# First attention's bias rows by one product, and another order of exponentials, scores and taps, in a two-block transformer kernel

## The chip, the cores and the metric

The kernel runs on one core of one Trainium2 chip. The metric is the device time of one execution in microseconds (us). Before the change three runs took 2164.03, 2169.14 and 2170.22 us; their median is 2169.14 us.

## The reference

The reference computes two transformer blocks on 512 tokens of width 1024, in float32. The first block mixes a sliding-window attention (8 query heads, 2 key heads, blocks of 128 queries against at most 256 keys) with a gated causal convolution of 31 taps over 512 channels, then a feed-forward layer. The second block (sparse attention, spatial gating, a layer of 16384 experts) is not touched by the change. What matters here of the first block:

```python
bucket = t5_causal_bucket(jnp.maximum(dist, 0))
bias = rel_bias.astype(jnp.float32)[bucket]
...
s = jnp.where(valid[None, :, None, None], s + bias, -jnp.inf)
m = jnp.maximum(jnp.max(s, axis=-1, keepdims=True), sink)
p = jnp.exp(s - m)
denom = jnp.sum(p, axis=-1, keepdims=True) + jnp.exp(sink - m)
p = (p / denom).astype(v.dtype)
o = jnp.einsum("bnhgqk,bnkhd->bnqhgd", p, vb)
...
h = a * jax.nn.sigmoid(gate)
h = lax.conv_general_dilated(h, conv_dw[:, None, :], ...) + conv_dw_b
```

The bias of a head depends only on the distance of query and key, so one row of 384 values per head holds all of it, and a query's bias is that row shifted.

## The kernel before, in words

Activations are kept transposed, channels on partitions and the 512 tokens along the free axis, as a high and a low float32r half. Every weight comes in units of 512 KB, through a ring of three: SyncE loads a unit into `wraw` (L1001 to L1008), ScalarE casts the high half to `WH` (L1191, when the unit before the last has been begun), VectorE or GpSimd subtracts to get the low half `WL` (L2297, L1140), and TensorE does three matmuls for each 128 rows of it (L469, L472, L473). A unit of a projection has 8 times 3 matmuls of 512 tokens. Each engine runs its own list in order and waits on semaphores. PSUM has eight banks, handed out in turn by `take`: a bank is used again when the eighth product before it has been read.

**The order around the change, on TensorE.** The first three input projections (convolution gates and values of chunks 0 and 1) run by halves of the tokens. Then come the bias rows (L588), the value unit of chunk 1, two units each of chunks 2 and 3, keys, values, and four query units. Then attention (L661): scores of blocks 0 and 1; then for each of the four blocks the tap products of the last channel chunk (`last_chunk_taps`, 8, 8, 8 and 7 products with diagonal matrices), scores of the block after next, and `weighted_values`, which transposes the probabilities (L636) and multiplies them by the values (L645). Behind it the mean over channels (L682) begins the convolution's layer norm.

**The bias rows.** VectorE spreads the table `relb` (33 x 8) to `relbB` (33 x 8 x 128) at L1761, 128 copies for each head. TensorE multiplies, head by head, 128 equal columns with the one-hot matrix `oneh` (33 x 384) at L592: all 128 partitions get the row of that head. ScalarE copies each of the eight banks to `brow` (L1263), which lies in the buffer of the scores. SyncE waits for all eight, writes them to DRAM as `skew_rows` (L1026, 1536 KB), waits until they have landed, and reads them back into `biasT` with a step of one row less one element (L1029), which shifts the row of partition p by p. Only then does it issue the load of the seventh unit and those behind it.

**VectorE.** From the first projection on it runs the convolution of chunks 0 to 2, one tap an instruction (`tap`, L1776 on): taps of chunk 0 alone at first, then pairwise with the next chunk's. Before every sixth tap it makes the low half of one unit, for the ten units from chunk 2's gate to the last query unit. `gated` (L1767) multiplies a chunk's values by its gates first; for the last chunk, whose taps TensorE does, it comes early in chunk 1's second half. 77 taps come before attention, 16 inside it, four a block. In attention (L1808) VectorE's order is `logits` of block 0 (scaled scores plus bias L1821, maximum L1826), then for each block: `logits` of the next, `normalise` (L1838), the taps, the sum of the last chunk's taps (L1852, L1855), and the low half of the block before's output (L1845).

**ScalarE.** In attention (L1296), for each block: exponentials with their sums, head by head (L1302), the diagonal matrices for later taps (L1292), the copies of the transposed probabilities (L1311), and the output's high half (L1315). VectorE's `normalise` waits for the exponentials; TensorE's transposes wait for `normalise`; its weighted values wait for the copies.

Of the kernel before, what the change touches and what calls it, by code (L numbers as in the profile page):

```python
# [8 lines left out]
F32 = mybir.dt.float32  # L9
# [7 lines left out]
P = 128  # L17
T = 512
NT = T // P
# [13 lines left out]
KF = FF // P  # L33
SKEW = 3 * P

GR = 4
# [100 lines left out]
def block_pair_kernel(nc, A, onehot_rows, inv_freq, out):  # L137

    ctx = ExitStack()
    with ctx:  # L140
# [151 lines left out]
        with ExitStack() as sc:  # L292
            hpad = sb("hpad", [P, CC, TAPS - 1 + T], F32, sc)
            cacc = sb("cacc", [P, CC, T], F32, sc)
            sg = sb("sg", [P, 2, T], F32, sc)
            kk = sb("kk", [P, T], F32, sc)
            vT = sb("vT", [P, T], F32, sc)
            v1 = sb("v1", [P, NT, P], F32, sc)
            q1 = sb("q1", [P, 4, T], F32, sc)
            biasT = sb("biasT", [P, NH, 2 * P], F32, sc)  # L300
            sc1 = sb("sc1", [P, 2, NH, 2 * P], F32, sc)
            pT1 = sb("pT1", [P, NH, 2, P], F32, sc)
            sinkb = sb("sinkb", [P, NH], F32, sc)
            st1 = sb("st1", [P, 2, 8, NH], F32, sc)
            relb = sb("relb", [BUCKETS + 1, NH], F32, sc)
            relbB = sb("relbB", [BUCKETS + 1, NH, P], F32, sc)
            oneh = sb("oneh", [BUCKETS + 1, SKEW], F32, sc)
            cln = sb("cln", [P, 2, T], F32, sc)
# [3 lines left out]
        TAP_GROUPS = [(0, 8), (8, 16), (16, 24), (24, TAPS)]  # L312
        brow = sc1[:, :, :, :].rearrange("p a h n -> p (a h n)")[:, 0:NH * SKEW].rearrange("p (h n) -> p h n", h=NH)
        skew_dram = nc.dram_tensor("skew_rows", (P, NH, SKEW), F32).ap()

# [135 lines left out]
        def _(pe):  # L451
# [136 lines left out]
            def bias_rows():  # L588
                pe.wait_ge(s("relb_spread"), 1)
                for h in range(NH):  # L590
                    out = take("brow", h)
                    full(pe.matmul(out[:, 0:SKEW], relbB[:, h, :], oneh[:, :], start=True, stop=True), "brow", h)  # L592

# [33 lines left out]

            def weighted_values(b):
                kts = [1] if b == 0 else [0, 1]
                pe.wait_ge(s("probs"), b + 1)  # L630
                for i in range(NH // 2):
                    out = take("pT", b, i)
                    for j in range(2):
                        for kt in kts:
                            w = (kt if b else 0) * P
                            mm = pe.transpose(out[:, (2 * j + kt) * P:(2 * j + kt + 1) * P],  # L636
                                              sc1[:, b % 2, 2 * i + j, w:w + P], ident[:, :])
                    full(mm, "pT", b, i)
                out = take("o", b)
                for h in range(NH):  # L640
# [20 lines left out]
            def attention():  # L661
                scores(0)
                scores(1)
                for b in range(NT):
                    last_chunk_taps(b)
                    if b + 2 < NT:
                        scores(b + 2)
                    weighted_values(b)
# [332 lines left out]
        def _(sp):  # L1001
# [21 lines left out]

            for h in range(NH):
                wait_read(sp, ("brow", h))
            sp.dma_start(skew_dram, brow[:, :, :]).then_inc(s("skew_out"), 16)  # L1026
            sp.wait_ge(s("skew_out"), 16)
# [149 lines left out]
        def _(act):  # L1177
# [82 lines left out]
            def bias_rows():  # L1260
                for h in range(NH):
                    src = wait_full(act, ("brow", h))
                    act.activation(brow[:, h, :], src[:, 0:SKEW], ACT.Copy).then_inc(frees(("brow", h)), 1)  # L1263

# [31 lines left out]
            def attention():  # L1296
                for b in range(NT):
                    w = P if b == 0 else 2 * P
                    st = st1[:, b % 2]
                    act.wait_ge(s("sink_gap"), b + 1)  # L1300
                    for h in range(NH):
                        act.activation(sc1[:, b % 2, h, 0:w], sc1[:, b % 2, h, 0:w], ACT.Exp, bias=st[:, 1, h:h + 1],  # L1302
                                       accum_out=st[:, 2, h:h + 1])
                    act.activation(st[:, 4, :], st[:, 3, :], ACT.Exp).then_inc(s("exps"), 1)
                    last_chunk_diags()
                    for i in range(NH // 2):
# [356 lines left out]
        def _(dve):  # L1663
# [82 lines left out]
            def prepare():  # L1746
# [13 lines left out]
                dve.wait_ge(s("relb_landed"), 32)  # L1760
                dve.tensor_copy(relbB[:, :, :], relb[:, :].unsqueeze(2).to_broadcast([BUCKETS + 1, NH, P])).then_inc(  # L1761
                    s("relb_spread"), 1)

            def convolution():
# [29 lines left out]
                alone = TAPS // 2  # L1794
                for w in range(alone):
                    tap(0, w)
                for c in range(CC - 2):
                    for w in range(alone, TAPS):
                        tap(c, w)
                        if w - alone < alone:  # L1800
                            tap(c + 1, w - alone)
                        if c == CC - 3 and w == alone:
                            gated(CC - 1)
                for u in beside:
                    low(u, s("w_beside"))
                return lambda w: tap(CC - 2, w), range(alone, TAPS)

            def attention(tap, taps_left):  # L1808
# [50 lines left out]
                for b in range(NT):  # L1859
                    if b + 1 < NT:  # L1860
                        logits(b + 1)
                    normalise(b)
                    for w in taps_left[b * len(taps_left) // NT:(b + 1) * len(taps_left) // NT]:
                        tap(w)
                    last_chunk(b)
# [592 lines left out]
```

## Time and profile before

| what | value |
|---|---|
| median of 3 runs | 2169.14 us |
| lowest and highest run | 2164.03, 2170.22 us |
| span of the profiled execution | 2161.6 us (its own time is not listed apart) |
| TensorE busy | 2121.7 us, 98% of the span |
| VectorE, GpSimd, ScalarE busy | 1442.4, 1038.6, 858.3 us |
| mean granted TensorE clock | 0.996 of 2.4 GHz |

The span runs from the first to the last instruction of the profiled execution. TensorE's busy time counts matmuls whose ends are modelled, so that it reads high; where it waits, and at which clock it runs, tells more than its share. DVE is VectorE, ACT is ScalarE, PE is TensorE, POOL is GpSimd, SPq is SyncE's queue.

### The profile page before, as it was taken

The numbers are of one execution on the slowest core, as the hardware profiler recorded it, in microseconds if no ns is written. First come the engines' busy times: TensorE is split into PE (matmuls) and PEld (weight loads), VectorE is DVE, ScalarE is ACT, GpSimd is POOL, SyncE is SP. The second block draws the span as 40 slices with busy tenths as digits, with TensorE's granted clock in tenths as the row PEclk, the third lists the DMA queues.
The fourth block names the chain that finished last, engine by engine and source line by source line (L and its number), as shares of the span: only waits on it lengthen the run. The fifth ranks groups of instructions, "written<-read, shape, count | busy, mean of one in ns | idle before, by whom it ended". The sixth has DMA issues, their size and how long they took to land.

```text
span 2161.6 us, 29125 instructions
## 1 busy us (share of the span) xinstructions
PE 2121.7 (98%) x10648; PEld 1837.8 (85%) x10648; DVE 1442.4 (67%) x2713; ACT 858.3 (40%) x1306; POOL 1038.6 (48%) x573
## 2 busy tenths in 40 slices
PE   8989999999999999999999999999999999999999
PEld 7857888888877877899999999999998888888887
DVE  5973411110054995369998777787867999999987
ACT  4354522232264454253334444444433333333332
POOL 1203244443423333435566888888863444444342
PEclk9999999999999999999999999999999999999999
DMA  4202344444442222334347899998899999999996
GB/s 177 82 27 62 104 117 127 117 119 115 117 118 74 86 71 77 117 106 121 112 147 207 242 267 321 284 315 249 261 309 318 388 388 371 373 375 377 369 359 251
DMA packets 240489, 444.14 MB, mean 205 GB/s; under 512 B 102459, under 2 KB 152028, under 8 KB 240220
## 3 DMA queue, kind: packets, MB, share of 16 engines
q1 hardware_dynamic: 152060, 299.07, 41.8%
q0 software_dynamic: 55488, 134.83, 19.3%
q10 hardware_dynamic: 32800, 8.39, 1.8%
q8 instruction: 85, 1.39, 0.3%
q14 instruction: 56, 0.46, 0.1%
HBM read 397.71 MB, written 44.50 MB: 205 GB/s over the span
## 4 chain that ended last, share of the span: by engine, by line
PE 69%; POOL 13%; DVE 8%; issue 4%; DMA 3%; ACT 2%; SPq 0%; DVEq 0%; ACTq 0%; POOLq 0%
PE bank L469 22%; PE bank L473 22%; PE bank L472 22%; POOL gate_matrices L1151 9%; POOL y L1160 4%; DMA y<-in_peer_u_rows,gidx 3%; DVE m L1979 1%; PE bank L923 1%; DVE xn L1980 1%; DVE WL L2297 1%; PE bank L645 1%; DMA wraw<-in_peer_u 1%; ACT sc L1302 1%; DVE y L2308 0%; DVE hots L2329 0%
## 5 line engine op out<-in xcount | busy, mean ns | idle before, releaser
L1140 POOL TENSOR_TENSOR WL<-wraw,WH 128x1024 fp32r<-128x1024 f32 x171 | 435.9, 2552 | 723.5 <-ACT WH L1191 723.5
L1191 ACT ACTIVATE WH<-wraw 128x1024 fp32r<-128x1024 f32 x411 | 435.0, 1060 | 627.4 <-PE bank L469 393.6
L469 PE MATMUL bank<-XH,WH 128*128 128x384 f32 (+2 forms) x1864 | 668.8, 359 | 12.6 <-DVE WL L2297 7.8
L473 PE MATMUL bank<-XH,WL 128*128 128x384 f32 (+2 forms) x1864 | 657.8, 353 | 0.0
L472 PE MATMUL bank<-XL,WH 128*128 128x384 f32 (+2 forms) x1864 | 657.6, 353 | 0.0
L469 PEld LDWEIGHTS bank<-XH,WH 128*128 128x128 f32 x1864 | 351.4, 189 | 46.3 <-issue 12.9
L472 PEld LDWEIGHTS bank<-XL,WH 128*128 128x128 f32 x1864 | 351.6, 189 | 29.0 <-issue 0.7
L473 PEld LDWEIGHTS bank<-XH,WL 128*128 128x128 f32 x1864 | 351.1, 188 | 28.7
L2297 DVE TENSOR_TENSOR WL<-wraw,WH 128x1024 fp32r<-128x1024 f32 x240 | 293.0, 1222 | 57.6 <-ACT WH L1191 51.8
L469 PE MATMUL bank<-WH,GH 128*128 128x512 f32 x768 | 298.9, 389 | 1.6 <-issue 1.6
L473 PE MATMUL bank<-WH,GL 128*128 128x512 f32 x768 | 298.8, 389 | 0.0
L472 PE MATMUL bank<-WL,GH 128*128 128x512 f32 x768 | 298.8, 389 | 0.0
L1160 POOL DMA_INDIRECT y<-in_peer_v,gidx x128 | 185.2, 1447 | 220.7 <-DVE hN L2316 203.0
L1151 POOL DMA_INDIRECT gate_matrices<-scat_gate,scat_at x128 | 243.7, 1904 | 40.9 <-issue 38.4
L2308 DVE CUSTOM_DVE_ANT_0 y<-y,x_nat 128x1024 f32<-128x1024 f32 x128 | 156.0, 1223 | 108.6 <-DMA y<-in_peer_u_rows,gidx 103.4
L1160 POOL DMA_INDIRECT y<-in_peer_u_rows,gidx x128 | 169.3, 1323 | 106.1 <-DVE gdot L2308 77.0
L469 PEld LDWEIGHTS bank<-WH,GH 128*128 128x128 f32 x768 | 144.1, 188 | 32.3 <-issue 2.3
L473 PEld LDWEIGHTS bank<-WH,GL 128*128 128x128 f32 x768 | 144.1, 188 | 29.9
L472 PEld LDWEIGHTS bank<-WL,GH 128*128 128x128 f32 x768 | 144.2, 188 | 29.8
L2316 DVE SCALAR_TENSOR_TENSOR hN<-y,gdot,hN 128x1024 f32<-128x1024 f32 x128 | 163.9, 1280 | 3.6 <-DMA y<-in_peer_v,gidx 0.6
L1589 ACT ACTIVATE ac<-bank 128x384 f32<-128x384 f32 x122 | 59.8, 490 | 239.0 <-PE bank L473 223.6
L1904 DVE TENSOR_TENSOR y<-bank,y 128x512 f32<-128x512 f32 x22 | 15.2, 692 | 208.2 <-PE bank L473 208.2
(313 smaller groups left out, 2561.8 us busy)
## 6 DMA issues: line engine op xcount, KB each, us to landing
wraw<-in_peer_u SPq DMA_DIRECT2D x128, 512.0 KB
wraw<-in_peer_v SPq DMA_DIRECT2D x128, 512.0 KB
activations<-ac SPq DMA_DIRECT2D x122, 192.0 KB
ar<-activations SPq DMA_DIRECT2D x122, 192.0 KB
gr<-gate_matrices SPq DMA_DIRECT2D x124, 128.0 KB
wraw<-in_w_gate SPq DMA_DIRECT2D x22, 512.0 KB
wraw<-in_w_up SPq DMA_DIRECT2D x22, 512.0 KB
wraw<-in_w_down SPq DMA_DIRECT2D x22, 512.0 KB
```

The lines of the kernel that those rows point to most:

```text
L469: mm = pe.matmul(out, wh, xh, start=first, stop=False)
L472: pe.matmul(out, wh, xl, start=False, stop=False)
L473: return pe.matmul(out, wl, xh, start=False, stop=last)
L645: mm = pe.matmul(out[half, (h % 4) * P:(h % 4 + 1) * P], v1[:, b - 1 + kt, half], pT1[:, h, kt, :], start=kt == kts[0], stop=kt == 1)
L1140: pool.tensor_tensor(WL[:, u % NW, 0:m], wraw[:, u % NR, 0:m], WH[:, u % NW, 0:m].bitcast(F32), ALU.subtract).then_inc(s("w_lo"), 1)
L1151: pool.indirect_dma_start(out=gate_cells[:, :], out_offset=bass.IndirectOffsetOnAxis(ap=scat_at[:, k:k + 1], axis=0), in_=scat_gate[:, k:k ...
L1160: pool.indirect_dma_start(out=gathered[:, row % NGATHER, :], out_offset=None, in_=(u_rows if row < HS else v_rows)[:, :], in_offset=bass.I ...
L1191: act.activation(WH[:, u % NW, 0:k * n], wraw[:, u % NR, 0:k * n], ACT.Copy).then_inc(s("w_hi"), 1)
L1589: act.activation(ac[:, x % NAC, :] if x < SENT else kept[:, x - SENT, :], src[:, 0:TD], ACT.Gelu_apprx_tanh).then_inc(frees(("a", x)), 1)
L2297: dve.tensor_tensor(WL[:, u % NW, 0:k * n], wraw[:, u % NR, 0:k * n], WH[:, u % NW, 0:k * n].bitcast(F32), ALU.subtract).then_inc(made, 1)
L2308: dve.tensor_tensor_reduce(out=at, in0=at, in1=x_nat[:, :], scale=1.0, scalar=0.0, op0=ALU.mult, op1=ALU.add, accum_out=gdot[:, row:row + ...
L2316: dve.scalar_tensor_tensor(out=hN[:, NTD, :], in0=at, scalar=gdot[:, row - HS:row - HS + 1], in1=hN[:, NTD, :], op0=ALU.mult, op1=ALU.add) ...
```

## The change

The table is spread to 33 x 16 x 8, so that 128 columns hold all eight heads sixteen times. One product gives the row of head h on every partition 8c + h, one copy brings it to `brow` (128 x 384), and one DMA writes each partition's row eight times, to fill the same 128 x 8 x 384 array in DRAM; the read back is as before. In attention, ScalarE runs the exponentials of block b + 1 before its other work of block b. TensorE transposes the probabilities of block b before the scores of block b + 2. VectorE does 66 single taps before attention and 27 inside it (6, 7, 7 and 7), and gates the last channel chunk after the 37th tap. Seven PSUM banks fewer are taken.

```diff
-            relbB = sb("relbB", [BUCKETS + 1, NH, P], F32, sc)
+            relbB = sb("relbB", [BUCKETS + 1, P // NH, NH], F32, sc)
...
-        brow = sc1[:, :, :, :].rearrange("p a h n -> p (a h n)")[:, 0:NH * SKEW].rearrange("p (h n) -> p h n", h=NH)
+        brow = sc1[:, 0, 0:2, :].rearrange("p h n -> p (h n)")[:, 0:SKEW]
...
-                for h in range(NH):
-                    out = take("brow", h)
-                    full(pe.matmul(out[:, 0:SKEW], relbB[:, h, :], oneh[:, :], start=True, stop=True), "brow", h)
+                out = take("brow", 0)
+                full(pe.matmul(out[:, 0:SKEW], relbB[:, :, :].rearrange("b c h -> b (c h)"), oneh[:, :], start=True, stop=True), "brow", 0)
...
                 for b in range(NT):
                     last_chunk_taps(b)
+                    turned_weights(b)
                     if b + 2 < NT:
                         scores(b + 2)
                     weighted_values(b)
...
-            for h in range(NH):
-                wait_read(sp, ("brow", h))
-            sp.dma_start(skew_dram, brow[:, :, :]).then_inc(s("skew_out"), 16)
+            wait_read(sp, ("brow", 0))
+            sp.dma_start(skew_dram.rearrange("(r c) h n -> (c h) r n", r=NH),
+                         brow.unsqueeze(1).to_broadcast([P, NH, SKEW])).then_inc(s("skew_out"), 16)
...
-                for h in range(NH):
-                    src = wait_full(act, ("brow", h))
-                    act.activation(brow[:, h, :], src[:, 0:SKEW], ACT.Copy).then_inc(frees(("brow", h)), 1)
+                src = wait_full(act, ("brow", 0))
+                act.activation(brow, src[:, 0:SKEW], ACT.Copy).then_inc(frees(("brow", 0)), 1)
...
-                for b in range(NT):
+                def exps(b):
...
+                exps(0)
+                for b in range(NT):
+                    if b + 1 < NT:
+                        exps(b + 1)
                     last_chunk_diags()
...
-                dve.tensor_copy(relbB[:, :, :], relb[:, :].unsqueeze(2).to_broadcast([BUCKETS + 1, NH, P])).then_inc(
+                dve.tensor_copy(relbB[:, :, :], relb[:, :].unsqueeze(1).to_broadcast([BUCKETS + 1, P // NH, NH])).then_inc(
                     s("relb_spread"), 1)
...
-                for w in range(alone):
-                    tap(0, w)
+                order = [(0, w) for w in range(alone)]
                 for c in range(CC - 2):
                     for w in range(alone, TAPS):
-                        tap(c, w)
+                        order.append((c, w))
                         if w - alone < alone:
-                            tap(c + 1, w - alone)
-                        if c == CC - 3 and w == alone:
-                            gated(CC - 1)
+                            order.append((c + 1, w - alone))
+                order += [(CC - 2, w) for w in range(alone, TAPS)]
+                for n, (c, w) in enumerate(order[:TAPS_BEFORE]):
+                    tap(c, w)
+                    if n == TAPS_BEFORE - 30:
+                        gated(CC - 1)
                 for u in beside:
                     low(u, s("w_beside"))
-                return lambda w: tap(CC - 2, w), range(alone, TAPS)
+                return tap, order[TAPS_BEFORE:]
```

`TAPS_BEFORE` is 66. `turned_weights` is the first half of the old `weighted_values`: the wait for the probabilities and the transposes.

## Rows read from the trace of the kernel before

**Rows 1.** The page: its first line, and the chain that ended last by engine.

```profile
span 2161.6 us, 29125 instructions
...
PE 69%; POOL 13%; DVE 8%; issue 4%; DMA 3%; ACT 2%; SPq 0%; DVEq 0%; ACTq 0%; POOLq 0%
```

**Rows 2.** Busy time by stretch: length, each engine, clock, DMA share, GB/s.

```profile
60.00:103.24 43.24, 43.23 (x193) 35.47 (x191) 43.20 (x63) 15.52 (x29) 8.65 (x1) 1.00 0.27 86
103.24:165.60 62.36, 55.17 (x295) 35.49 (x295) 44.80 (x67) 31.76 (x106) 5.21 (x2) 0.97 0.08 26
```

**Rows 3.** The chain in order of time, 0 to 300 us: start, length, what.

```profile
32.43 7.55 PE bank L592 x16
39.98 0.72 PE bank L469
40.70 0.43 PE bank L472
...
45.81 0.24 PE bank L472
...
103.26 0.61 ACT q L1280
...
165.62 3.63 PE bank L682 x8
```

**Rows 4.** Busy time by microsecond around the bias products, columns as in rows 2.

```profile
34.00:35.00 1.00, 1.00 (x4) 0.56 (x3) 1.00 (x2) 0.84 (x2) 0.00 (x0) 1.00 0.09 25
...
36.00:37.00 1.00, 1.00 (x3) 0.60 (x2) 0.96 (x2) 0.49 (x1) 0.00 (x0) 0.50 0.00 0
```

**Rows 5.** ScalarE's timeline: start, length, instruction, idle before it and releaser.

```profile
33.30 0.49 ACT L1263 ACTIVATE sc<-bank 128x384 f32<-128x384 f32 x1 [0.24 <-PE bank L592]
...
52.78 1.06 ACT L1191 ACTIVATE WH<-wraw 128x1024 fp32r<-128x1024 f32 x1 [10.92 <-DMA wraw<-in_w_in]
```

**Rows 6.** SyncE's timeline: the write of the bias rows.

```profile
40.60 0.33 SPq L1026 DMA_DIRECT2D skew_rows<-sc  x1
```

**Rows 7.** DMA issues: size, median us from issue to landing.

```profile
skew_rows<-sc SPq DMA_DIRECT2D x1, 1536.0 KB, 5.1
...
biasT<-skew_rows SPq DMA_DIRECT2D x1, 1024.0 KB, 5.8
```

**Rows 8.** VectorE's timeline: two low halves, and the last taps before attention.

```profile
64.10 1.21 DVE L2297 TENSOR_TENSOR WL<-wraw,WH 128x1024 fp32r<-128x1024 f32 x1
...
69.21 1.21 DVE L2297 TENSOR_TENSOR WL<-wraw,WH 128x1024 fp32r<-128x1024 f32 x1
...
91.91 12.01 DVE L1786 SCALAR_TENSOR_TENSOR cacc<-hpad,taps,cacc 128x512 f32<-128x512 f32 x18
```

**Rows 9.** Waits from 103 to 165.6 us: in total, times, longest.

```profile
DVE st L1835 <- ACT st L1304: 12.1, 3, 5.7
```

**Rows 10.** Groups from 103 to 165.6 us: busy, mean ns, idle before.

```profile
L657 PE MATMUL bank<-hpad,xn 128*128 128x512 f32 x32 | 14.3, 598 | 0.0
...
L1786 DVE SCALAR_TENSOR_TENSOR cacc<-hpad,taps,cacc 128x512 f32<-128x512 f32 x18 | 13.4, 749 | 0.4
...
L645 PE MATMUL bank<-pT,v 128*64 128x128 f32 x112 | 12.7, 295 | 1.7 <-DVE sc L1821 1.7
...
L1302 ACT ACTIVATE sc<-sc,st 128x256 f32<-128x256 f32 x24 | 11.8, 495 | 0.0
...
L1821 DVE SCALAR_TENSOR_TENSOR sc<-bank,biasT 128x512 f32<-128x512 f32 x14 | 8.7, 683 | 3.3 <-PE bank L636 1.9 <-PE bank L624 1.5
L636 PE MATMUL bank<-ident,sc 128*128 128x128 f32 x56 | 7.4, 279 | 4.6 <-DVE cacc L1852 1.8 <-DVE sc L1838 1.7 <-DVE XL L1845 1.1
L1838 DVE TENSOR_TENSOR sc<-sc,st 128x2048 f32<-128x2048 f32 x3 | 6.9, 2291 | 0.1
...
L624 PE MATMUL bank<-kk,q 64*128 64x256 f32 x48 | 6.5, 391 | 0.0
```

**Rows 11.** Busy time by two microseconds in block 0, columns as in rows 2.

```profile
122.00:124.00 2.00, 2.00 (x9) 1.36 (x6) 1.97 (x2) 0.71 (x2) 0.00 (x0) 0.50 0.03 8
```

More of the change, by code:

```diff
@@ L34 @@
 SKEW = 3 * P
+TAPS_BEFORE = 66
 GR = 4
@@ L626, in scores, with turned_weights @@
                     full(mm, "sc", b, i)
-            def weighted_values(b):
+            def turned_weights(b):
                 kts = [1] if b == 0 else [0, 1]
@@ L638, in weighted_values @@
                     full(mm, "pT", b, i)
+            def weighted_values(b):
+                kts = [1] if b == 0 else [0, 1]
                 out = take("o", b)
@@ L1862, in attention @@
                     normalise(b)
-                    for w in taps_left[b * len(taps_left) // NT:(b + 1) * len(taps_left) // NT]:
-                        tap(w)
+                    for c, w in taps_left[b * len(taps_left) // NT:(b + 1) * len(taps_left) // NT]:
+                        tap(c, w)
                     last_chunk(b)
```

## The prediction

> **What bounds the kernel now.** I began with the span and the chain of work that ended last [rows 1]: TensorE holds 69% of it, and the rest are hand-overs between stages that follow one another. The change touches only the first 166 us. Everything behind that needs the first block's result, so microseconds won there arrive at the end whole, if nothing there runs by a clock of its own. I looked for such a thing (a long prefetch, a fixed stream) and found none: weights go through a ring of three buffers, and no load runs further ahead than that.
>
> Next, the busy time by stretch [rows 2]. From 60 to 103.2 us TensorE is busy all the time (43.23 of 43.24 us): the input projections are bound by products and by nothing else. From 103.2 to 165.6 us (first attention) it is busy 55.17 of 62.36 us, so some 7 us wait there. Then the chain in order of time [rows 3]: the bias products hold TensorE for 7.55 us, and the unit behind them starts in steps of 0.43 us a matmul where later ones take 0.23 us. The windows of one microsecond [rows 4] say why: the granted clock is 1.00 (2.4 GHz) until two thirds of the bias products are through and 0.50 (1.2 GHz) from 36 us on. The products read 33 rows of the array, most of them zeros; while nothing else runs, the clock falls, and the dense unit behind, begun at 39.98 us, pays until 45.81.
>
> **Part 1: one bias product for eight.** Eight products in 7.55 us are four at the full clock, one across the fall and three at half. One at the full clock takes 7.55 / (4 + 1.4 + 3 x 2) = 0.66 us, an estimate that the spacing of the evictions bears out. TensorE thus reaches the next unit at 33.1 instead of 40.0 us: **6.9 us**, straight on the path, since TensorE doesn't wait again until 103 us.
>
> **Part 2: the clock.** With 0.66 us of thin work between dense units I expect no fall. The unit begun at 39.98 us has (45.81 - 39.98) / 0.43, 13 whole matmuls, before a step of 0.23 to 0.24 is reached [rows 3]: 13 x 0.20 = **2.6 us**. Ends: 0 (the clock falls all the same) and 2.6.
>
> **Part 3: evictions, spread and store.** Seven ScalarE copies of 0.49 us go [rows 5]; ScalarE then idled for 10.9 us on a load, so this alone is worth nothing. VectorE's spread of the bias table shrinks eightfold, in front of an idle stretch: nothing. The DMA still writes 1536 KB, now as 1024 pieces of 1.5 KB out of one repeated row, instead of 128 runs of 12 KB. No row shows that form. The nearest two: the write of today, 5.1 us, and the skewed read back, 1024 pieces of 1 KB, 5.8 us for 1024 KB with weights flowing beside it [rows 7]. I take 5.1 us, as bytes, direction and target are those of today's write; ends 5.1 and 9 us (the second is the read's rate per byte, 5.8 x 1.5).
>
> **Part 4: whether the weights keep up.** This is the cover that part 1 uses. SyncE's queue is in order: it waits for the evicted bias rows, issues the write at 40.60 us [rows 6], waits the 5.1 us for it, issues the read at 45.7, and only then the seventh unit's load, which ScalarE casts at 52.78 us [rows 5], 7.1 us after the read; VectorE subtracts next, in 1.21 us [rows 8]. All of it moves up: product done at 33.1, copied at 33.8, write issued 33.9, landed 39.0, read and load issued, load landed 46.1, cast until 47.1, subtracted by 48.4. TensorE, at 24 matmuls x 0.23 = 5.5 us a unit, wants that unit at 33.1 + 3 x 5.5 = 49.6 us. Spare: **1.2 us**. After it VectorE makes one unit's low part every 5.11 us (64.10 to 69.21 [rows 8]), faster than 5.5, so the spare grows, less about 1.3 us for each gating that falls between. Gating the last channel chunk earlier (after the 37th tap, about 65 us) finds its projection, the fifth unit behind the bias product, done by 60.6 us; no wait. So 0 us is lost if the write takes up to 6.3 us; at 9 us TensorE loses 2.7, say 3 us, and I keep that as the end.
>
> **Part 5: fewer taps ahead of attention.** VectorE does 66 instead of 77 single taps before attention. Today it ends them at 103.9 (91.91 + 12.01 [rows 8]), just behind TensorE. With TensorE 9.6 us earlier (93.7) the old 77 would have ended near 98: TensorE's scores would have stood 4 us. With 66 it ends near 91. The price: 27 taps lie inside attention, not 16, some 8 us of VectorE more.
>
> **Part 6: the order inside attention.** Today [rows 9, 10]: ScalarE runs a block's exponentials (8 x 0.49 us) only when the block before is finished, and VectorE stands 12.1 us for them. TensorE idles 4.6 us before transposes and 1.7 us before weighted values, released by VectorE. I walked the three queues with these durations: transposes 0.49 us per bank, values 0.82 per head pair, scores 0.53 per bank, 0.86 per tap product, VectorE 0.64 per logits tile, 2.29 each for maximum and normalisation, 0.67 (12.01 / 18 [rows 8]) or 0.75 us per tap, as it is paired with another accumulator or not, and bank reuse by eighth predecessor. Without the change the walk puts the end of attention at 165.2; the trace has 165.6 [rows 3]. With it, counted from the same start:
> - block 0: probabilities are ready 1.0 us after the tap products end; the fourth scores bank waits 2.2 us for VectorE's six taps and sum (bank reuse). End 0.6 us earlier.
> - block 1: its exponentials are already done, so VectorE never waits; its block is now 4 logits, maximum, normalisation, 7 taps, sum and low half, 14 us, about TensorE's 15. Scores 3 wait 1.2 us for the low half. End 2.0 us earlier.
> - blocks 2 and 3: transposes start directly behind tap products. Ends 2.5 and then **3.5 us** earlier.
> Ends: a gain of 0 if VectorE's extra 8 us bind, and 5 if the waits that remain (5.0 us in the walk, 0.6 of them at the start) are partly rounding. 3.5 is what the walk gives.
>
> The clock in attention: a stretch of scores, transposes and values, all thin, precedes each group of tap products, and the first fell to 0.50 at 122 to 124 us [rows 11]. I carry it over unchanged. Against the change speaks a rule of the Trainium skill, page "TensorE: Matmul & The Clock Gate", Part 4 (PE-mode transpose), that transposes don't count as a busy engine in the way that matmuls do; by it, transposes and scores side by side would lower the clock oftener. The rows agree once in four blocks and no more.
>
> **Sum.** 6.9 + 2.6 + 3.5 = 13.0 us off the profiled span of 2161.6: 2148.6. That execution's own time isn't listed; its span lies 7.5 us under the median run of 2169.14, so I take the difference from the median: **2156 us**. The three runs shown spread over 6.2 us; that goes into the range.
>
> **Rivals.**
> A. *The first two parts hold, attention gives nothing* (VectorE is now its bound, or the clock falls in more blocks: each fall of some 3 us at half costs up to 1.5 us). For: only 1 us a block separates VectorE from TensorE in the walk. Against: VectorE's 12.1 us of waiting is more than the 8 us of taps it takes on. -9.5 us: 2159.6. Chance 0.17.
> B. *The clock falls, or the seventh unit comes late*: the store needs 9 us. -13 + 3 = -10: 2159, and with A about 2162.5. Chance 0.12, a quarter of it with A.
> C. *The bias store runs on few DMA engines* since its pattern repeats a row, and the weights queue behind it; this is the way to a slower kernel. If one of sixteen did all of it, the write would take up to 16 x 5.1 = 82 us: TensorE would stand from 49.6 until 33.9 + 82 + 7.1 + 2.3 = 125 us, and -13 + 76 = +63: 2232. It decides from a write of about 5.1 + 1.2 + 13 = 19 us on. Against it: the pattern still has 128 partitions as its outer dimension on both sides, like both transfers of today. The Trainium skill, page "DMA: Bandwidth & Descriptors", "Why a DMA increments its semaphore by 16 and not by 1", lets the slowest dimension of either side decide how many engines share a transfer; by it all 16 do, and C falls away. No row of before shows a repeated row. Chance 0.03.
> D. *The gain doesn't reach the end*: an indirect gather or a weight stream further on sets its own time. The chain has 13% on GpSimd [rows 1], but its start hangs on the expert choice, which moves along. -3 us or less: 2167. Chance 0.05.
>
> **How the numbers follow.** Forecast 0.63, A 0.17, B 0.12, C 0.03, D 0.05. A measurement of this kernel tells 0.3%, 6.5 us, from no change. The forecast, A and B alone lie above that; D, and A with B at its bad end, are the same; C is slower. With some noise of runs: faster 0.89, same 0.08, slower 0.03. The range: upward it takes in A, B and half of the runs' spread (2162), downward a gain of 15 us (attention at 5) and 3 us of spread less a little for both at once (2151 to 2150).
>
> **What would show it.** One bias product of 0.65 us and the next unit at 33 us with 0.23 us steps; granted clock 1.00 from 32 to 100 us; the write landing in 5 to 6 us and the seventh unit's subtraction ending before 49.6; TensorE busy throughout 60 to 93.7; VectorE idle for 2 to 3 us ahead of the first logits, at about 94; no VectorE wait for exponentials behind block 0; the column-mean product near 152.6 us. I am wrong if TensorE waits for a low part between 45 and 93, if two or more tap groups run at half clock, or if what lies behind 165.6 us doesn't shift as one.

## The result, and the profile after

Four runs of the changed kernel took 2146.53 to 2154.46 us, median 2151.14; the kernel before took 2164.03 to 2170.22 beside them, median 2167.05. The ratio is 0.9923 with a 95% interval of 0.9900 to 0.9947. A second measurement (below) gave 0.9942, 0.9920 to 0.9964. The forecast was 2156 us, 13.0 us less than before; the two medians differ by 15.9 and, in the second measurement, by 12.6 us. The profiled execution took 2146.53 us, the shortest of the four, with a span of 2144.8.

The chain of work in order of time, for the same stretch as [rows 3] (start, length, what; lines behind the change have moved by a few):

```profile
32.76 0.84 PE bank L592 x2
33.60 0.43 PE bank L470
34.03 0.23 PE bank L473
...
94.19 0.60 ACT q L1283
...
110.78 1.65 PE bank L624 x4
112.43 2.59 PE bank L648 x16
...
152.40 3.63 PE bank L686 x8
```

One bias product stands where eight stood, and the step to 0.23 us is reached with the next unit's second matmul. ScalarE's last query copy, which I call mark A, starts at 94.19 instead of 103.26 us; the column-mean product, mark B, at 152.40 instead of 165.62. So 9.1 us come from the projections and 4.1 from attention (58.2 us from A to B instead of 62.4), 13.2 in all. The window that answers to [rows 4] keeps its clock:

```profile
36.00:37.00 1.00, 1.00 (x6) 0.84 (x5) 0.96 (x2) 0.00 (x0) 0.00 (x0) 1.00 1.02 366
```

The stages by busy time, as in [rows 2] (second: A to B):

```profile
60.00:94.19 34.19, 34.15 (x153) 27.96 (x151) 34.15 (x43) 13.36 (x27) 5.69 (x2) 1.00 0.35 109
94.19:152.33 58.14, 55.04 (x294) 36.20 (x295) 52.07 (x78) 31.56 (x106) 0.00 (x0) 0.97 0.06 19
```

TensorE has the same 55 us of work in attention as before; of its waits 3.1 us are left, where there were 7.2. VectorE is now busy for 52.07 of 58.14 us, where it had 44.80 of 62.36. Its waits for exponentials (12.1 us in [rows 9]) are gone, and the groups of [rows 10] show TensorE's idle time before transposes down from 4.6 to 0.6 us, before weighted values from 1.7 to 0. A new wait of 1.6 us stands before the fourth group of scores, for a bank that VectorE frees:

```profile
L648 PE MATMUL bank<-pT,v 128*64 128x128 f32 x112 | 12.6, 295 | 0.0
...
L624 PE MATMUL bank<-kk,q 64*128 64x256 f32 x48 | 8.1, 404 | 1.6 <-DVE cacc L1862 1.6
...
L636 PE MATMUL bank<-ident,sc 128*128 128x128 f32 x56 | 6.8, 274 | 0.6 <-DVE sc L1848 0.6
```

The store, as in [rows 7], took 6.4 us instead of 5.1, the read back 5.4 instead of 5.8. ScalarE cast the seventh unit at 47.21 us (52.78 in [rows 5]), and VectorE waited 0.95 us for the first scores of attention, so its taps were done in time. From each engine's list of instructions:

```profile
skew_rows<-sc SPq DMA_DIRECT2D x1, 1536.0 KB, 6.4
biasT<-skew_rows SPq DMA_DIRECT2D x1, 1024.0 KB, 5.4
...
47.21 1.06 ACT L1195 ACTIVATE WH<-wraw 128x1024 fp32r<-128x1024 f32 x1 [12.03 <-DMA wraw<-in_w_in]
...
96.30 1.29 DVE L1831 SCALAR_TENSOR_TENSOR sc<-bank,biasT 128x512 f32<-128x512 f32 x2 [0.95 <-PE bank L624]
```

Behind B the profiled span was another 3.6 us shorter (1992.4 instead of 1996.0). The marks agree to 0.1 us for a long way: the feed-forward layer, the second projections and the expert scores all begin 13.2 us earlier. The difference arises after 1100 us, where one VectorE instruction beside a GpSimd one took 4.49 us in the profile of before and 2.29 in this one, and in a stretch of half clock near 1210 us that the profile of before has and this one lacks. The change doesn't reach there; an experiment below treats it as chance.

### The profile page after: what moved, and what is told of

It is laid out like the page before. It is cut to its first block, busy times and chain, and to the rows that moved or that the text cites. A ratio compares the mean times of both kernels' runs of the same rounds, so it can differ in the third digit from the quotient of the medians.

```text
span 2144.8 us, 29086 instructions
## 1 busy us (share of the span) xinstructions
PE 2112.6 (98%) x10634; PEld 1833.4 (85%) x10634; DVE 1442.9 (67%) x2713; ACT 852.5 (40%) x1299; POOL 1031.0 (48%) x573
## 4 chain that ended last, share of the span: by engine, by line
PE 70%; POOL 16%; DVE 6%; issue 4%; DMA 2%; ACT 1%; SPq 0%; DVEq 0%; ACTq 0%; POOLq 0%
PE bank L470 22%; PE bank L474 22%; PE bank L473 22%; POOL gate_matrices L1155 11%; POOL y L1164 5%; DMA y<-in_peer_u_rows,gidx 1%; PE bank L660 1%; DVE m L1989 1%; PE bank L927 1%; DMA wraw<-in_peer_u 1%; DVE xn L1990 1%; PE bank L648 1%; PE bank L864 0%; PE bank L519 0%; DVE isc L1990 0%
## 5 line engine op out<-in xcount | busy, mean ns | idle before, releaser
L1144 POOL TENSOR_TENSOR WL<-wraw,WH 128x1024 fp32r<-128x1024 f32 x171 | 428.5, 2509 | 717.4 <-ACT WH L1195 717.4
L1155 POOL DMA_INDIRECT gate_matrices<-scat_gate,scat_at x128 | 251.2, 1962 | 39.0 <-issue 39.0
L1164 POOL DMA_INDIRECT y<-in_peer_u_rows,gidx x128 | 162.5, 1269 | 100.7 <-DVE gdot L2318 71.0
L2326 DVE SCALAR_TENSOR_TENSOR hN<-y,gdot,hN 128x1024 f32<-128x1024 f32 x128 | 163.9, 1281 | 3.8 <-DMA y<-in_peer_v,gidx 0.8
L1597 ACT ACTIVATE ac<-bank 128x384 f32<-128x384 f32 x122 | 59.8, 490 | 250.8 <-PE bank L474 232.8
```

What stands on the lines that cost most here:

```text
L1144: pool.tensor_tensor(WL[:, u % NW, 0:m], wraw[:, u % NR, 0:m], WH[:, u % NW, 0:m].bitcast(F32), ALU.subtract).then_inc(s("w_lo"), 1)
L1155: pool.indirect_dma_start(out=gate_cells[:, :], out_offset=bass.IndirectOffsetOnAxis(ap=scat_at[:, k:k + 1], axis=0), in_=scat_gate[:, k:k ...
L1164: pool.indirect_dma_start(out=gathered[:, row % NGATHER, :], out_offset=None, in_=(u_rows if row < HS else v_rows)[:, :], in_offset=bass.I ...
L1597: act.activation(ac[:, x % NAC, :] if x < SENT else kept[:, x - SENT, :], src[:, 0:TD], ACT.Gelu_apprx_tanh).then_inc(frees(("a", x)), 1)
L2326: dve.scalar_tensor_tensor(out=hN[:, NTD, :], in0=at, scalar=gdot[:, row - HS:row - HS + 1], in1=hN[:, NTD, :], op0=ALU.mult, op1=ALU.add) ...
```

## Experiments

All traces are read at marks A and B, because a few microseconds are seen there to 0.1 us and in the total hardly at all.

In the table B is the start of its first matmul, up to 0.1 us before the chain's entry. A moved between 93.3 and 94.4 us among runs whose code up to it does the same, so A to B is the column to compare. The marks of a row are from one trace.

| run | A | A to B | B | time, ratio to before |
|---|---|---|---|---|
| before | 103.3 | 62.3 | 165.6 | 1 |
| changed | 94.2 | 58.1 | 152.3 | 0.9923 (0.9900 to 0.9947) |
| changed_again | 94.4 | 58.0 | 152.4 | 0.9942 (0.9920 to 0.9964) |
| bias_only | 93.8 | 70.1 | 163.9 | 0.9987 (0.9967 to 1.0006) |
| attn_only | 100.2 | 58.0 | 158.2 | 0.9967 (0.9950 to 0.9985) |
| taps77 | 94.3 | 62.7 | 157.0 | 0.9967 (0.9947 to 0.9987) |
| late_exps | 93.5 | 67.0 | 160.5 | 0.9974 (0.9954 to 0.9994) |
| scores_first | 93.3 | 60.0 | 153.3 | one run |
| sum_first | 94.3 | 59.7 | 154.0 | 0.9946 (0.9926 to 0.9965) |
| taps72_pool_late | 93.4 | 60.1 | 153.5 | 0.9965 (0.9945 to 0.9986) |
| thin8 | 101.8 | 59.8 | 161.6 | one run |
| rows33_8 | 103.4 | 58.1 | 161.5 | one run |
| dense8 | 98.8 | 58.2 | 157.0 | one run |
| store_twice | 102.1 | 59.7 | 161.8 | one run |

### The bias part alone

The kernel before with the hunks on `relbB`, `brow`, the product, the eviction and the store, and none of the others:

```diff
...
-                for h in range(NH):
-                    out = take("brow", h)
-                    full(pe.matmul(out[:, 0:SKEW], relbB[:, h, :], oneh[:, :], start=True, stop=True), "brow", h)
+                out = take("brow", 0)
+                full(pe.matmul(out[:, 0:SKEW], relbB[:, :, :].rearrange("b c h -> b (c h)"), oneh[:, :], start=True, stop=True), "brow", 0)
...
```

> The kernel before with the bias part alone: one product, one eviction, the repeated-row store; attention's order and the 77 single taps ahead of it stay. Mark A is the start of ScalarE's last query copy (103.26 us before, 94.19 after), mark B the start of the column-mean product (165.62 before, 152.40 after). Theory 1 (the parts lean on each other: VectorE's taps don't shrink when TensorE gets earlier): A at 94 to 94.5, VectorE ends its 77 taps only at 98 to 103, the first logits wait for that, and the stage from A to B grows from 62.4 to 65 to 69 us; B at 159 to 163.5, so only 2 to 6.5 us of the 9.1 us arrive. Rival 2 (the parts are independent): A at 94.2, stage 62.4, B at 156.6, 9 us arrive.

VectorE's timeline in this run: its last 18 taps ahead of attention, and the first logits right behind them; then TensorE's first transposes.

```profile
85.77 16.28 DVE L1784 SCALAR_TENSOR_TENSOR cacc<-hpad,taps,cacc 128x512 f32<-128x512 f32 x18
...
101.98 1.28 DVE L1819 SCALAR_TENSOR_TENSOR sc<-bank,biasT 128x512 f32<-128x512 f32 x2
...
111.80 1.54 PE L635 MATMUL bank<-ident,sc 128*128 128x128 f32 x6 [4.61 <-DVE sc L1836]
```

A came 9.5 us earlier, and at B 1.7 us of them were left; the time can't be told from no change. TensorE waited 4.61 us for the first block's probabilities, which the taps had held up, and ran at half clock from about 110 to 120 us and from 134 to 137. Theory 1 holds, and even its worse end (69 us) was too mild by 1.1 us: it had the wait and not the clock. The parts aren't independent.

### The attention part alone

The changed kernel with the bias hunks undone:

```diff
...
-                out = take("brow", 0)
-                full(pe.matmul(out[:, 0:SKEW], relbB[:, :, :].rearrange("b c h -> b (c h)"), oneh[:, :], start=True, stop=True), "brow", 0)
+                for h in range(NH):
+                    out = take("brow", h)
+                    full(pe.matmul(out[:, 0:SKEW], relbB[:, h, :], oneh[:, :], start=True, stop=True), "brow", h)
...
```

> The changed kernel with the old bias part (eight products, eight evictions, contiguous store). Theory 1: A stays at 103.3, VectorE is done with its 66 taps at 96 to 100 and waits; the stage from A to B takes 58.2 us as in the changed kernel, B at 161.5, 4.2 us saved. Rival 2 (the new order gains only when TensorE arrives early): stage at 61 to 62.4, at most 1 us saved.

The stage took 58.0 us, as in the changed kernel: the new order doesn't need an early TensorE. (Its clock didn't fall at all inside attention here; in the first trace of the changed kernel it fell once.) But A came at 100.2, not 103.3, with the same eight products. The chain and the clock by microsecond (columns as in [rows 2]) say why:

```profile
32.60 5.35 PE bank L593 x16
```

```profile
38.00:39.00 1.00, 1.00 (x3) 0.82 (x4) 0.96 (x2) 0.92 (x2) 0.00 (x0) 0.58 0.00 0
...
41.00:42.00 1.00, 1.00 (x5) 0.80 (x4) 0.96 (x3) 0.00 (x0) 0.00 (x0) 0.71 0.93 393
```

The fall came at 38 us, when the products were through (5.35 us instead of 7.55), and was over at 42. The bias part was therefore worth 9.1 us against one execution of before and 6.0 against this one: where the clock falls, and for how long, differs from run to run.

### Taps ahead of attention

```diff
-TAPS_BEFORE = 66
+TAPS_BEFORE = 77
...
-                    if n == TAPS_BEFORE - 30:
+                    if n == 36:
```

> The changed kernel with 77 single taps ahead of attention instead of 66 (16 inside instead of 27); everything else as changed. Theory 1: VectorE would be the late one; its taps end 11 x 0.67 = 7.4 us later, at about 102.7 instead of 95.35; the first logits start there instead of at 96.3, and the stage from A to B grows by 1.6 us (if the taps end at 98.4) to 6 us (at 102.7); B at 154 to 158.5. Rival 2 (fewer taps ahead bring nothing, as they are paid inside attention): B at 152.4 or earlier.

The first logits started at 102.92 us, as computed, and B came 4.7 us later. TensorE stood 7.1 us for the first block's probabilities, and its clock fell to 0.50 during that wait. So the smaller number of taps is what lets 4.7 of the bias part's microseconds through. VectorE's last 18 taps again took 16.28 us, 4.3 more than the 12.01 of [rows 8]; two of them are the reason, below.

### Exponentials early

```diff
-                exps(0)
                 for b in range(NT):
-                    if b + 1 < NT:
-                        exps(b + 1)
+                    exps(b)
```

> The changed kernel with ScalarE's old order (a block's exponentials only when the block before is finished); TensorE's and VectorE's lists stay as changed. Theory 1: this piece carries the stage; VectorE stands 9 to 12 us for exponentials again, and since it now has 27 taps inside, the walk of the queues gives a stage of 64 us instead of 58.2: B at 158, 5.6 us slower than the changed kernel. Rival 2 (the transposes' place carries it): stage at most 60 us.

B came 8.2 us later, the stage took 8.9 us longer (67.0); the expectation was 5.6 and 64. The wait is back:

```profile
DVE st L1843 <- ACT st L1307: 11.4, 3, 4.4
```

This is the largest piece of the attention part. Some of the 3 us beyond the walk are the clock: it fell in two blocks here (about 110.5 to 114 and 128 to 131 us), in the changed kernel in one at most. In the time it is 0.9974, against 0.9923 and 0.9942.

### Transposes ahead of scores

```diff
-                    turned_weights(b)
                     if b + 2 < NT:
                         scores(b + 2)
+                    turned_weights(b)
```

> The changed kernel with TensorE's old order in a block (scores of the block after next ahead of the transposes); exponentials early and 66 taps as changed. Theory 1: the transposes' place is the smallest piece; with old places the fourth scores bank and then the transposes wait for VectorE's sum (bank reuse), the walk gives a stage of 59.8 us instead of 58.1, B 1.7 us later. Rival 2 (it is the piece that carries the stage): 3 us or more later.

The stage took 60.0 us, 1.9 longer; the walk gave 59.8. TensorE's timeline has the waits of before back, at the bank that the sum frees and at the weighted values:

```profile
109.93 0.44 PE L636 MATMUL bank<-ident,sc 128*128 128x128 f32 x2 [2.43 <-DVE cacc L1862]
111.22 2.88 PE L648 MATMUL bank<-pT,v 128*64 128x128 f32 x16 [0.86 <-DVE sc L1831]
```

### What lowers the clock

Seven further products stand in front of the real one, into the same bank, and are overwritten by it. Only their operands differ; each run has one of the three lines, in this order:

```diff
                 out = take("brow", 0)
+                for _ in range(NH - 1):
+                    pe.matmul(out[:, 0:SKEW], relbB[:, :, :].rearrange("b c h -> b (c h)"), oneh[:, :], start=True, stop=True)
...
+                    pe.matmul(out[:, 0:SKEW], hN[0:BUCKETS + 1, 0, 0:P], hN[0:BUCKETS + 1, 1, 0:SKEW], start=True, stop=True)
...
+                    pe.matmul(out[:, 0:SKEW], hN[:, 0, 0:P], hN[:, 1, 0:SKEW], start=True, stop=True)
```

> The changed kernel with seven more copies of the bias product in front of the real one, into the same bank and unread; one eviction, one store as changed. Theory 1 (thin products lower the clock): the group takes about 7.5 us instead of 0.84, the granted clock falls to 0.50 during it and the unit behind pays for several us, so that mark A (start of ScalarE's last query copy) comes 8 to 10 us later than the 94.2 us of the changed kernel. Rival 2 (the eight evictions and banks did it, not the products): the clock stays at 1.00, the group takes 8 x 0.64 = 5.1 us, A 4.5 us later.

> As the run with seven more bias products, but the seven extra ones multiply 33 rows of the input x, so no zeros. Theory 1a (few rows lower the clock): falls as with the bias products, A 8 to 10 us later than 94.2. Theory 1b (the zeros of the one-hot matrix lower it): clock stays at 1.00, A 4.5 us later.

> As before, but the seven extra products are full, 128 rows of the input x by 384 columns. Theory 1: the clock stays at 1.00, the group takes 8 x 0.64 = 5.1 us, A 4.5 us later than 94.2. Rival 2 (any float32 product lowers the clock): A 8 to 10 us later.

The windows of two microseconds of the three runs, in this order:

```profile
38.00:40.00 2.00, 2.00 (x5) 0.85 (x4) 1.93 (x3) 0.65 (x2) 0.00 (x0) 0.50 0.00 0
40.00:42.00 2.00, 2.00 (x6) 1.61 (x5) 1.12 (x2) 0.90 (x1) 0.00 (x0) 0.50 0.70 274
```

```profile
38.00:40.00 2.00, 2.00 (x4) 0.67 (x2) 1.93 (x3) 0.00 (x0) 0.00 (x0) 0.50 0.00 0
40.00:42.00 2.00, 2.00 (x5) 1.38 (x5) 0.06 (x1) 1.26 (x2) 0.00 (x0) 0.50 0.05 18
```

```profile
38.00:40.00 2.00, 2.00 (x9) 1.58 (x9) 1.93 (x3) 1.55 (x2) 0.00 (x0) 1.00 0.17 64
40.00:42.00 2.00, 2.00 (x11) 1.63 (x10) 2.00 (x3) 0.00 (x0) 0.00 (x0) 1.00 1.01 369
```

Full products kept 2.4 GHz, and A came 4.6 us later, which is their own time (4.5 expected). 33 rows of real numbers brought 1.2 GHz and 9.2 us; 33 rows of the one-hot matrix brought it and 7.6 us, a little below its 8 to 10. The zeros aren't needed: few rows are enough. Evictions and banks play no part, since each run has one. Each is a single trace, but the others agree: the clock fell between 35 and 38.5 us in all four traces with eight products of 33 rows in a row (`before`, `attn_only`, `thin8`, `rows33_8`), and stayed at 1.00 from 32 to 48 us in all nine with one.

### The spare behind the store

```diff
             sp.wait_ge(s("skew_out"), 16)
+            sp.dma_start(skew_dram.rearrange("(r c) h n -> (c h) r n", r=NH),
+                         brow.unsqueeze(1).to_broadcast([P, NH, SKEW])).then_inc(s("skew_out"), 16)
+            sp.wait_ge(s("skew_out"), 32)
```

> The changed kernel with the repeated-row store issued twice, one after the other, before the read back. It prices the spare behind the store. In the changed kernel the seventh unit's subtraction ends at 49.53 us and TensorE begins that unit at about 49.9, so 0.4 us are spare. Theory 1: the load lands 6.4 us later, TensorE stands 6.0 us before that unit, and A comes at about 100.2 instead of 94.2; B the same 6 us later or a little less. Rival 2 (loads or casts have slack that hides it): TensorE stands under 3 us.

TensorE's timeline at the seventh unit, and the windows around it:

```profile
55.23 0.77 PE L470 MATMUL bank<-XH,WH 128*128 128x512 f32 x1 [4.88 <-DVE WL L2310]
```

```profile
52.00:54.00 2.00, 0.00 (x0) 0.00 (x0) 0.14 (x1) 1.23 (x2) 0.00 (x0) 0.94 1.03 414
54.00:56.00 2.00, 0.77 (x2) 0.70 (x3) 2.00 (x3) 1.25 (x2) 0.00 (x0) 0.50 0.14 55
56.00:58.00 2.00, 2.00 (x6) 1.52 (x6) 2.00 (x4) 1.06 (x1) 0.00 (x0) 0.50 0.89 250
```

The second store took 5.7 us, the cast came at 52.77 instead of 47.21, and TensorE stood 4.88 us for the low half. Then the clock fell while it stood, and the next unit paid: A came 7.9 us later, not 6.0. The load has no slack beyond the last microsecond, so theory 1 holds for the wait; it left out what a wait of this length does to the clock. B came 9.5 us later, where 6 or a little less was expected: the fall of the clock inside attention was longer here, and the stage took 59.7 us.

### Is the gain behind B real

> The changed kernel once more, with more rounds on the chip of the run beside it. Its first four runs stood 15.9 us below the kernel before, while the marks in the traces give 13.2 us up to the column-mean product and 3.5 us behind it. If those 3.5 us are chance (the stretch behind the column mean took from 1992 to 2004 us in the traces so far, whatever the change), the ratio comes out at 0.9940, 13 us; if the change reaches behind the stage, it stays at 0.9923 or below, 16.6 us.

The second measurement gave 0.9942, and its profiled execution spent 2154.0 - 152.4 = 2001.6 us behind B, where the first spent 1992.4. The kernel before spent 1996.0, and `rows33_8`, whose code behind B is that of the changed kernel, 1992.3. Over all fourteen traces the stretch behind B, in which no run's code differs in what it does, took 1992 to 2014 us. So the 3.6 us behind B are within chance; the two intervals overlap, and both hold 0.9940.

### Two attempts to beat it

In the first, VectorE takes block 0's sum before its taps, and ScalarE copies the transposed probabilities before it makes diagonal matrices:

```diff
                     normalise(b)
+                    if b == 0:
+                        last_chunk(b)
...
-                    last_chunk(b)
+                    if b:
+                        last_chunk(b)
...
-                    last_chunk_diags()
                     for i in range(NH // 2):
...
+                    last_chunk_diags()
                     src = wait_full(act, ("o", b))
```

> A version meant to beat the changed kernel: in block 0 VectorE takes the sum of the last chunk's taps before its six single taps (it frees the bank that the fourth scores group waits for), and ScalarE copies the transposed probabilities before it makes the next diagonal matrices. In the changed kernel TensorE stands 1.62 us for that bank and reaches the column-mean product 58.1 us after mark A. Theory 1 (TensorE's own work and that wait carry the stage): the wait goes, block 1 gives part of it back to the wait for the low half, stage 57.2 us, B 0.9 us earlier. Rival 2 (VectorE carries the stage, it idles only 0.37 us in it before its last block): stage 58.1 as now; the wait only moves to block 1. In the time neither can be told from no change.

```profile
107.34 2.10 PE L624 MATMUL bank<-kk,q 64*128 64x256 f32 x16
...
124.75 1.89 PE L624 MATMUL bank<-kk,q 64*128 64x256 f32 x8 [2.92 <-DVE XL L1855]
```

The wait in block 0 went and came back in block 1, nearly twice as long: the third scores group there needs the bank that VectorE's low half frees, and VectorE's list is no shorter. The stage took 59.7 us, 1.6 more than as changed. The second theory was right that VectorE carries it, and neither had the loss. The loss is as large as what a fall of the clock cost: from about 125 to 128.4 us it stood at 0.50, right behind that wait, so that eight matmuls of scores took 1.89 us and block 1's weighted values 4.21, where the repeated run of the changed kernel, at full clock, has 1.14 and 3.33. Whether the fall comes in every execution isn't known. In the time it equals the changed kernel (0.9946 against 0.9942).

The second attempt rests on two taps of the changed kernel that took 2.88 us instead of 0.74. VectorE's first of them, and GpSimd's two instructions:

```profile
86.35 2.88 DVE L1794 SCALAR_TENSOR_TENSOR cacc<-hpad,taps,cacc 128x512 f32<-128x512 f32 x1
```

```profile
85.51 3.17 POOL L1144 TENSOR_TENSOR WL<-wraw,WH 128x1024 fp32r<-128x1024 f32 x1 [54.45 <-ACT WH L1195]
90.95 2.53 POOL L1144 TENSOR_TENSOR WL<-wraw,WH 128x1024 fp32r<-128x1024 f32 x1 [2.27 <-ACT WH L1195]
```

```diff
-TAPS_BEFORE = 66
+TAPS_BEFORE = 72
...
+                if u == BESIDE_TAPS.stop:
+                    pool.wait_ge(s("exps"), 1)
...
-                    if n == TAPS_BEFORE - 30:
+                    if n == 36:
```

> A version meant to beat the changed kernel, and a test of a collision: GpSimd makes its first two low halves behind attention's first exponentials instead of at 85.5 and 90.95 us, and VectorE does 72 taps ahead of attention instead of 66 (5, 5, 5 and 6 inside). In the changed kernel two of VectorE's last taps took 2.88 us instead of 0.74, each beside one of those GpSimd instructions, so that the 66 taps ended at 95.35 us. Theory 1 (the GpSimd instructions held VectorE up): no tap over 0.8 us, the 72 taps end at about 95.1, the first logits start at 96.3 as now, and with fewer taps inside the walk gives a stage of 57.2 instead of 58.1 us, B at 151.4. Rival 2 (the long taps have another cause, and VectorE is at its limit): 72 taps end near 99.4, the first logits there, stage 59 to 61 us, B 1 to 3 us later. In the time theory 1 can't be told from the changed kernel (1 us), rival 2 hardly.

```profile
85.51 8.70 DVE L1796 SCALAR_TENSOR_TENSOR cacc<-hpad,taps,cacc 128x512 f32<-128x512 f32 x13
95.56 1.29 DVE L1833 SCALAR_TENSOR_TENSOR sc<-bank,biasT 128x512 f32<-128x512 f32 x2 [1.35 <-PE bank L624]
...
103.32 1.02 DVE L1839 TENSOR_TENSOR st<-st,sinkb 128x8 f32<-128x8 f32 x1
104.38 2.27 DVE L1840 TENSOR_SCALAR st<-st 128x8 f32<-128x8 f32 x1
```

Thirteen taps took 8.70 us, none of them long, and VectorE was ready before the scores: the GpSimd instructions had held it up. But GpSimd now ran from 101.97 to 106.62 us, and there two of VectorE's smallest instructions, 0.17 us each otherwise, took 1.02 and 2.27, each until one of GpSimd's two had ended. TensorE stood 3.58 us for the probabilities of block 0, its clock fell to 0.50 from 108 us on, and the stage took 60.1 us. The first theory is right about the cause and wrong about the gain: the collision moved along with the instruction, to a worse place. By mark B the changed kernel stays the best of those run; in the time the version with the early sum can't be told from it.

## Why the prediction was right, and where it was lucky

**Part 1, one product.** 6.9 us were forecast. The next unit began at 33.60 instead of 39.98 us, 6.4 earlier, though everything had started 0.3 us later in this execution: 6.7.

**Part 2, the clock.** Forecast 2.6; the rest of the difference at A is 9.07 - 6.38 = 2.7. The cause is shown by the three runs with seven products more, and by the nine traces with one product, in which the clock stayed. The size isn't a property of the kernel: the run with the old bias part met a short and late fall, and there parts 1 and 2 together are worth 6.0 us and not 9.5. My lower end of 0 for part 2 allowed for it, but part 1 hangs on the same draw (5.35 us for the products instead of 7.55), and the text took 6.9 for certain.

**Part 3, the store.** Forecast 5.1 us with ends of 5.1 and 9; measured 6.4, and 5.9 and 5.7 in the run that stored twice. This is the term that was mis-sized. Its form explains 0.6 us of it: issued at 38.7 us or later, the repeated row took 5.7 us in four stores, the old form, issued at 38.57 us in the run with the old bias part, 5.1. Issued near 34 us, as in the changed kernel, it took 5.9 to 6.4; why the earlier moment costs more, no run here shows.

**Part 4, the spare.** 1.2 us forecast, 0.4 left: the cast came at 47.21, the subtraction ended at 49.53, and TensorE took the unit without a wait. The store took 1.3 us more than forecast, and that is where the 0.8 us went. The point from which the store decides was therefore about 6.8 us, near the 6.3 of the text, and beyond it its price is more than one for one: with two stores a wait of 4.88 us cost 7.9. Rival B, which came within half a microsecond, was likelier than the 0.12 it was given.

**Part 5, the taps.** The mechanism is right: with 77 taps B is 4.7 us later. But VectorE ended its 66 taps at 95.35 and not near 91, and had 0.95 us to spare and not 2 to 3. (The first logits start 2.1 us behind mark A, before as after, so at 96.30 us and not at about 94.) The step that failed is the tap's duration, taken from a stretch where GpSimd had lost: VectorE ran the 18 taps of [rows 8] in 12.01 us, while GpSimd's subtraction beside them took 11.54 us, until the taps were through at 103.9 (the next one took 2.35):

```profile
94.59 11.54 POOL L1140 TENSOR_TENSOR WL<-wraw,WH 128x1024 fp32r<-128x1024 f32 x1 [63.86 <-ACT WH L1191]
```

In the changed kernel GpSimd won twice, at 2.14 us each.

**Part 6, the order.** Forecast 3.5, measured 4.1. Block by block, transposes 2 and 3 began directly behind the tap products, and the waits at probabilities (0.63) and at the fourth scores group (1.62) were there, where the walk had 1.0 and 2.2. The wait for the low half in block 1 (walk: 1.2) was 1.26 us in the repeated run and absent in the first, in which TensorE ran some of block 0 at half clock; the stage took 58 us in both. The pieces tested alone followed the walk in direction, exponentials dearer than it had them (8.2 us at B instead of 5.6), transposes right (1.9 us of stage, where 1.7 were expected).

**The clock in attention.** One fall, in block 0, in the first trace of the changed kernel, as before; none in the repeated one. The Trainium skill's statement that transposes don't count as activity ("TensorE: Matmul & The Clock Gate", Part 4) would have made it worse in the changed order; neither trace of the changed kernel has more than the one of before, so nothing here supports that price.

**The rivals.** A: attention did give its part, though VectorE is nearly its bound. C: nothing of it, the store took 6.4 us where the prediction's estimate for one engine of sixteen was 82, and the 16 engines' mean busy share was 1.02 in the window from 36 to 37 us. D: the 13.2 us stay whole through the first 1100 us. Behind that the first trace gains 3.6 us more, so what lies behind 165.6 us did not shift as one; by the prediction's own words that was a sign of being wrong, and only the spread of the other traces makes it chance. What I hadn't put among the rivals is that the parts need each other. The marks show it: alone the bias part brings B 1.7 us earlier, and the attention part shortens its stage by 4.3, together they bring 13.2. The times agree (0.13%, interval to zero and beyond, and 0.33%; together 0.6 to 0.8%), but their intervals alone wouldn't tell it.

**Luck.** The first median, 2151.14 us, stood some 15.9 us under before where 13.0 were forecast, at the low end of the range (2151 to 2150); 3.6 us of that in the profiled execution lie behind B, which the change doesn't reach. The second measurement gave 12.6. And the 9.1 us at A met the forecast 9.5 because the profile of before had a long fall of the clock: against the short one of the run with the old bias part it would have been 6.0.

## What to carry to other kernels

When TensorE gets earlier, ask which engine's list was timed against it: here 7.8 of 9.5 us were lost at the next meeting with the old order and the old number of taps, and 4.7 of 13.2 with the old number of taps alone. A row of products over few rows can cost as much again through the clock as in its own time (seven cost 9.2 us where seven full ones cost 4.6); one alone between dense units left the clock at 2.4 GHz in all nine traces. And a duration read beside another engine's work holds only for who won there.

## What the runs showed of the hardware that I had not expected

- A VectorE tap (two operands in SBUF) and a GpSimd subtraction don't run side by side, one waits. The loser varies: GpSimd took 11.54 us instead of 2.4 in the profile of before and 5.42 in the run with the old bias part, both times until VectorE's taps were through; a VectorE tap took 2.88 instead of 0.74 in that of after, and two VectorE instructions on 8 columns 1.02 and 2.27 instead of 0.17 where GpSimd had been put beside them (the slower of the two has one operand in SBUF, not two). This is the rule of the Trainium skill, page "SBUF — State Buffer", "Who interferes with whom": VectorE and GpSimd share a pair of ports, which one of them holds for a whole instruction. The traces agree; that one GpSimd instruction lost to some fourteen taps in a row goes beyond the page. What decides who wins, no run here shows.
- TensorE's clock fell from 2.4 to 1.2 GHz while it was busy all the time, in all four traces with eight products of 33 rows in a row, zeros or not (granted clock 0.50); with seven of 128 rows and one of 33 it stayed at 1.00. During a wait of 4.88 us it fell too.
- A fall isn't the same from run to run: with the same eight products, half clock lasted from about 35.5 to 45.7 us in one execution and from about 38 to 41.6 in another, which moved A by 3.1 us.
- A store from one repeated row of 1.5 KB a partition into DRAM took 5.7 to 6.4 us for 1536 KB in the twelve traces that have it, against 5.1 from 12 KB a partition in both others.
